# Strassen products in all three feed-forward blocks, their weight sums made by adding transfers

## The reference

```python
def conv_ffn(x, ln_g, up_w, conv_w, conv_b, down_w):          # blocks 0 and 1
    u = causal_dwconv(rms_norm(x, ln_g) @ up_w, conv_w, conv_b)   # 3 taps along the positions
    gate, up = u[..., :FFN_DIM], u[..., FFN_DIM:]
    return (jax.nn.silu(gate) * up) @ down_w

def swiglu(xn, w_gate, w_up, w_down):                          # block 2
    return (jax.nn.silu(xn @ w_gate) * (xn @ w_up)) @ w_down
```

## Time and profile before

| what | us |
|---|---|
| median of 3 runs | 2398.46 (2397.93 to 2400.35) |
| the profiled execution's own time | 2399.27 |
| its span | 2397.5 |
| PE busy | 2371.2 (99%) |
| DVE busy | 1484.8 (62%) |
| ACT busy | 1086.1 (45%) |
| POOL busy | 357.9 (15%) |
| transfers | 226.24 MB, mean 94 GB/s |

### The profile page before, as it was taken

One profiled execution on the slowest core, in us unless ns is written; L12 is line 12 of the kernel. 1 busy time (PEld: TensorE's weight loads), 2 busy tenths in 40 slices (PEclk: granted clock), 3 DMA queues, 4 the chain that ended last, 5 costly groups with the idle time before them and its releaser, 6 DMA issues.

```text
span 2397.5 us, 30764 instructions
## 1 busy us (share of the span) xinstructions
PE 2371.2 (99%) x11952; PEld 1944.2 (81%) x11952; DVE 1484.8 (62%) x2356; ACT 1086.1 (45%) x1878; POOL 357.9 (15%) x286
## 2 busy tenths in 40 slices
PE   8999999999999999999999999999999999999999
PEld 6677878888888877788888877787788878898987
DVE  6778776763666777766456547534655445873763
ACT  6654554442445677644234334324443334442433
POOL 0252252210111000122011100001210001100001
PEclk9999999999999999999999999999999999999999
DMA  4532223223223221232332332231234332233232
GB/s 164 109 93 79 80 70 99 97 86 108 97 83 120 75 76 49 73 108 92 93 106 87 91 131 84 71 102 57 72 123 136 115 106 79 81 105 99 95 97 89
DMA packets 74847, 226.24 MB, mean 94 GB/s; under 512 B 8144, under 2 KB 12368, under 8 KB 74576
## 3 DMA queue, kind: packets, MB, share of 16 engines
q1 hardware_dynamic: 70272, 215.90, 28.1%
q10 hardware_dynamic: 4432, 8.39, 2.0%
HBM read 215.87 MB, written 8.39 MB: 94 GB/s over the span
## 4 chain that ended last, share of the span: by engine, by line
PE 60%; DVE 1%; ACT 0%; issue 0%; DMA 0%; POOL 0%; POOLq 0%; DVEq 0%; ACTq 0%; SPq 0%
PE bank L1272 59%; PE bank L1276 1%; DVE t L2230 1%; DVE t L2233 1%; ACT t L1715 0%; DVE t L2241 0%; DMA t<-in_w 0%; POOL t L2877 0%; ACT t L1718 0%; ACT L1718 0%; DVE t L2237 0%; DVE t L2798 0%; POOLq L3100 0%; DVEq L3100 0%; DVE t L2644 0%
## 5 line engine op out<-in xcount | busy, mean ns | idle before, releaser
L1272 PE MATMUL bank<-t 128*128 128x512 f32 (+5 forms) x11526 | 2346.4, 369 | 19.1 <-DVE t L2233 7.9
L1272 PEld LDWEIGHTS bank<-t 128*128 128x128 f32 (+2 forms) x11526 | 1901.0, 186 | 433.3 <-issue 80.1
L1715 ACT ACTIVATE t<-t 128x1024 fp32r<-128x1024 f32 (+5 forms) x676 | 564.0, 847 | 564.6 <-PE bank L1272 276.6
L2230 DVE TENSOR_TENSOR t<-t 128x1024 fp32r<-128x1024 f32 (+7 forms) x774 | 687.3, 901 | 202.9 <-ACT t L1715 192.4
L1718 ACT ACTIVATE t<-t 128x512 f32<-128x512 f32 (+6 forms) x610 | 367.5, 616 | 455.8 <-DVE t L2230 307.1
L2877 POOL TENSOR_TENSOR t<-t 128x512 f32<-128x512 f32 (+4 forms) x206 | 316.3, 1542 | 1551.9 <-ACT t L1718 559.7
L2230 DVE TENSOR_TENSOR t<-bank,t 128x512 f32<-128x512 f32 (+4 forms) x434 | 279.2, 648 | 425.2 <-PE bank L1272 414.7
L2233 DVE SCALAR_TENSOR_TENSOR t<-t 128x512 f32<-128x512 f32 (+5 forms) x536 | 386.6, 733 | 102.3 <-ACT t L1718 63.8
L1715 ACT ACTIVATE t<-bank 128x512 f32<-128x512 f32 (+4 forms) x184 | 84.7, 477 | 205.4 <-PE bank L1276 146.9
L2880 POOL TENSOR_SCALAR t<-t 128x128 f32<-128x128 f32 (+3 forms) x64 | 40.9, 645 | 478.6 <-ACT t L1715 247.6
L2233 DVE SCALAR_TENSOR_TENSOR t<-bank,t 128x512 f32<-128x512 f32 x56 | 38.5, 688 | 68.8 <-PE bank L1272 68.8
(11 more groups left out here) (30 smaller groups left out, 53.0 us busy)
## 6 DMA issues: line engine op xcount, KB each, us to landing
t<-in_w SPq DMA_DIRECT2D x304, 512.0 KB, 3.4
t<-in_w SPq DMA_DIRECT2D x48, 384.0 KB, 3.0
t<-in_w SPq DMA_DIRECT2D x56, 320.0 KB, 3.0
t<-in_w SPq DMA_DIRECT2D x28, 256.0 KB, 2.8
tab<-t ACTq DMA_DIRECT2D x1, 2560.0 KB
t<-in_x SPq DMA_DIRECT2D x8, 256.0 KB, 5.0
t<-tab SPq DMA_DIRECT2D x8, 256.0 KB, 3.7
spill<-t ACTq DMA_DIRECT2D x1, 2048.0 KB, 8.3
```

The source lines that it names most:

```text
L1272: return eng.matmul(out, lhs, rhs, start=start, stop=stop, skip_group_check=loose)
L1715: return eng.activation(out, in_, ACT.Copy, scale=scale)
L2230: return eng.tensor_tensor(out, a, b, o)
```

## The change

- `QUADS` becomes a table: f = 9, 12, 14, 16, 18, 20 in blocks 0 and 1, and 10 of the 11 in block 2 (f = 5 becomes an ordinary pair). The sums of activations are made in each block (in XA for blocks 0 and 1).
- The order of the products becomes p1, p5, p6, p3, p7, p2, p4, and the four weight units are taken up at steps 0, 1, 3 and 5: first chunks (p1); s12 (p5, p6); s34 (p3, p7); last chunks (p2, p4). `cut_age` stays 2 throughout.
- Three of the four weight sums are made by transfers. A packed region of 128 x 2048 holds the four quarters. SP copies three of them (768 KB) into one of two buffers, 19 steps ahead (`base`). POOL issues a transfer that adds 512 KB from HBM into it, 15 steps ahead (`add1`), and one that adds 256 KB within SBUF, 9 steps ahead (`add2`). DVE makes the fourth sum, 128 x 512, 3 steps ahead (`add3`) in a buffer of its own, `sum4`. One of the two buffers is `scratch`, the memory of `acc` and `sqs`.
- The unit s34 lies in two buffers, so its `split` is two ACT copies of 512 elements and its `cut` two DVE subtractions of 512.
- In blocks 0 and 1 a Strassen pair's rows go through the taps; its results are multiplied by the row of norms on DVE, and gate times up is on DVE (11 steps after the pair's start; parts at 12 and 13).

```diff
-QUADS = (4, 5, 7, 8, 10, 12, 13, 15, 16, 18, 19)
-PRODUCTS = ("p1", "p2", "p6", "p5", "p7", "p3", "p4")
+QUADS = {0: (9, 12, 14, 16, 18, 20), 1: (9, 12, 14, 16, 18, 20), 2: (4, 7, 8, 10, 12, 13, 15, 16, 18, 19)}
+SUM_AGES = ((19, 15, 9, 3),) * 3
+PRODUCTS = ("p1", "p5", "p6", "p3", "p7", "p2", "p4")
+QUAD_HALF = {"p1": (0, 0), "p5": (1, 0), "p6": (1, 1), "p7": (2, 0), "p3": (2, 1), "p4": (3, 0), "p2": (3, 1)}
...
+        region = self.region((gate, 0, 4, gate_c + f * P, P), (up, 0, 4, up_c + f * P, P),
+                             (up, 4, 4, up_c + f * P, P), (gate, 4, 4, gate_c + f * P, P))
+        first = self.load(region, 0, S)
+        last = self.load(region, 2 * S, UNIT)
+        sources = (("raw", first, S), ("s12", (s, f), UNIT), ("s34", (s, f), UNIT), ("raw", last, UNIT))
         for i, product in enumerate(PRODUCTS):
-            if i % 2 == 0:
-                age, self.cut_age = self.cut_age, 1 if i == 4 else self.cut_age
-                u = self.ring(sources[i // 2])
-                self.cut_age = age
-                g.units.append(u)
-            self.put(Piece(g, i // 2, i, i + 1, i == 0))
+            if QUAD_HALF[product][0] == len(g.units):
+                g.units.append(self.ring(sources[len(g.units)]))
+            self.put(Piece(g, QUAD_HALF[product][0], i, i + 1, i == 0))
...
+        for name, age in zip(("base", "add1", "add2", "add3"), SUM_AGES[s]):
+            self.start(name, (s, f), t - age)
...
     def split(u):
-        copy(buf.his[u % N_W][:, 0:n], K.source(u)).then_inc(*sig["cut_hi"].up(u))
+        for a, b, of in K.source(u):
+            t = copy(buf.his[u % N_W][:, a:b], of)
+        t.then_inc(*sig["cut_hi"].up(u))
...
-            tt(buf.s1[:, S:UNIT], b[:, 0:S], b[:, S:UNIT], ADD).then_inc(*sig["sum1"].up(f))
-            tt(buf.s1[:, 0:S], a[:, 0:S], buf.s1[:, S:UNIT], ADD).then_inc(*sig["sum"].up(f, "s1"))
-            tt(buf.s2[:, 0:S], a[:, 0:S], b[:, 0:S], ADD)
-            tt(buf.s2[:, S:UNIT], a[:, S:UNIT], buf.s1[:, 0:S], ADD).then_inc(*sig["sum"].up(f, "s2"))
+            tt(buf.sum4[:, :], K.sums(sf)[:, 2 * S:3 * S], buf.raws[last % N_W][:, S:UNIT], ADD).then_inc(*sig["sum"].up(sf))
...
+    def adds(T):
+        for sf in at("add1", T):
+            region, *_ = plan.quad_units[sf]
+            i, turn, _ = K.sums_at(sf)
+            if turn > 1:
+                w.wait_ge(*sig.added[i][0].at(turn - 1))
+            w.wait_ge(*K.based(sf))
+            eng.dma_start(K.sums(sf)[:, 0:UNIT], K.region(region)[:, S:3 * S], accum_op=ADD).then_inc(
+                *sig.added[i][0].up())
+        for sf in at("add2", T):
+            i, turn, _ = K.sums_at(sf)
+            if turn > 1:
+                w.wait_ge(*sig.added[i][1].at(turn - 1))
+            w.wait_ge(*K.added(sf, 0))
+            eng.dma_start(K.sums(sf)[:, 2 * S:3 * S], K.sums(sf)[:, 0:S], accum_op=ADD).then_inc(*sig.added[i][1].up())
...
+    def base(sf):
+        region, *_ = plan.quad_units[sf]
+        i, turn, before = K.sums_at(sf)
+        if before:
+            w.wait_ge(*sig["cut"].at(plan.quad_units[before][4]))
+        elif i:
+            for j in range(4):
+                w.wait_ge(*sig["tee_lo"].at((sf[0], 3), j))
+        else:
+            w.wait_ge(*sig["lo"].at(*h_of(sf[0], 0)))
+        if turn > 1:
+            w.wait_ge(*sig.base[i].at(turn - 1))
+        eng.dma_start(K.sums(sf)[:, 0:3 * S], K.region(region)[:, 0:3 * S]).then_inc(*sig.base[i].up())
```

More of the change, by code:

```diff
@@ L293, in feat_steps, with quad @@
         self.pending.append(g)
[L295 to L299, removed]
+    def quad(self, s, f, gate, gate_c, up, up_c):
+        key = ("gu", s, f)
+        self.until(lambda: self.past("tees", (s, 3), 6 if f == QUADS[s][0] else SUM_AGES[s][0] + 4) and self.place(
+            [((*key, "b"), 0, 10), ((*key, "d"), 1, 6), ((*key, "a"), 5, 4)]), key)
@@ L528, in ffn @@
         late = 5 if s < 2 else 2
-        if s == 2:
-            for k in range(4):
-                self.once("tees", k, lambda k=k: self.past("rms", "n2", 3) and (k == 0 or self.past("tees", k - 1, 4)))
+        apart = 4 if s == 2 else 12
+        for k in range(4 if QUADS[s] else 0):
+            self.once("tees", (s, k), lambda k=k: self.past("rms", src, 3) and (
+                k == 0 or self.past("tees", (s, k - 1), apart)))
         self.start("ffn", s)
@@ L1114, in raw_read, with sums_at, sums, based @@
     def raw_read(self, r):
-        users = [u for u, (kind, n, _, _) in enumerate(self.plan.units) if kind == "raw" and n == r]
+        users = [u for u, (kind, n, _) in enumerate(self.plan.units) if kind == "raw" and n == r]
         done = [self.sig["cut"].at(u) for u in users]
-        for f, (first, *_) in self.plan.quad_units.items():
-            if r in (first, first + 1):
-                done.append(self.sig["sum"].at(f, "s2"))
-        return done
+        for sf, (_, last, *_) in self.plan.quad_units.items():
+            if r == last:
+                done.append(self.sig["sum"].at(sf))
+        return done
+    def sums_at(self, sf):
+        n, before = QUADS[sf[0]].index(sf[1]), [q for q in QUAD_LIST[:QUAD_LIST.index(sf)]]
+        turn = 1 + sum(QUADS[s].index(f) % 2 == n % 2 for s, f in before)
+        return n % 2, turn, (sf[0], QUADS[sf[0]][n - 2]) if n >= 2 else None
+    def sums(self, sf):
+        return self.buf.sums[self.sums_at(sf)[0]]
+    def based(self, sf):
+        i, turn, _ = self.sums_at(sf)
+        return self.sig.base[i].at(turn)
+    def added(self, sf, j):
+        i, turn, _ = self.sums_at(sf)
+        return self.sig.added[i][j].at(turn)
     def tee(self, i):
@@ L1308, in quads @@
         out = take(key)[:, 0:H2] if first else K.of(key)[:, 0:H2]
-        u, half = g.units[p.k0 // 2], p.k0 % 2
+        which, half = QUAD_HALF[product]
+        u = g.units[which]
         wh, wl = (t[u % N_W][:, half * S:half * S + S].rearrange("p (k n) -> p k n", k=4) for t in (buf.his, buf.los))
@@ L1936, in quads @@
[L1936 to L1946 removed]
+                copy(out, K.of(("gu", s, f, QUAD_BANK[product]))[:, 0:H2]).then_inc(*sig["q_copy"].up(s, f, product))
@@ L2287, in evacuate @@
             if s < 2:
-                if f >= 2 or (f == 1 and kind == "up"):
-                    w.wait_ge(*sig["tap"].at(("ga" if (n - 3) % 2 == 0 else "up", s, (n - 3) // 2), 2))
+                fu_free(n, s)
                 scaled(g, buf.fu[n % 3][:, 4:S + 4])
@@ new lines, in fu_free, with taps @@
+    def fu_free(n, s):
+        if n >= 3:
+            w.wait_ge(*sig["tap"].at(("ga" if (n - 3) % 2 == 0 else "up", s, (n - 3) // 2), 2))
+    def taps(key):
+        kind, s, f = key
+        n = 2 * f + (kind == "up")
+        ft = f + FFC * (kind == "up")
+        v, ub = buf.fv[n % 6], buf.fu[n % 3]
+        for k in (1, 2):
+            w.wait_ge(*(sig["tap0"].at(key) if k == 1 else sig["tap"].at(key, 1)))
+            stt(v[:, :], ub[:, 2 + k:S + 2 + k], pc(f"fcw{s}", 3 * ft + k), v[:, :], MUL, ADD).then_inc(
+                *sig["tap"].up(key, k))
@@ L3007, in gpsimd_program @@
         ssm(T)
+        adds(T)
         ffn(T)
@@ L3042, in sync_program @@
                 load(plan.units[u][1] + N_W)
+        for sf in at("base", T):
+            base(sf)
         for h in at("tb", T):
```

371 lines of the change are left out of this document (213 added, 158 removed).

## The result

| | before | after |
|---|---|---|
| median, us | 2398.85 (2397.93 to 2400.35, 4 runs) | 2432.97 (2429.82 to 2436.29, 4 runs) |
| ratio | | 1.0142, 95% interval 1.0124 to 1.0159 |
| the profiled execution's own time | 2399.27 | 2434.27 |
| its span | 2397.5 | 2432.2 |

The change makes the kernel 34.1 us slower. The direction was as predicted, the size three times the predicted 11.0 us, and 2433 lies outside the range (2390 to 2422). Two figures of the page after, against the earlier trace rows: PE's busy time should have fallen by 12 us and rose by 4.9; transfers by POOL's queue (the last line) are new.

A forecast was written before the change was run, and what follows sets the result against it. PE's own work was taken to bound the kernel; -12.1 + 5.5 + 0.4 + 15.2 + 2.0 = +11.0 us on 2399.3 gave 2410.3, or 2409.5 us as the median. The range was 2390 to 2422.

The forecast's parts named there:

- PE's own work: Strassen pairs of all blocks, 10.07 us against 10.90 for ordinary ones if nothing waits: -12.1 us.
- the sign that I had named: PE's busy time over the whole kernel falls by about 12 us while its idle time rises by over 20.
- The third weight unit: s34, needed at step 3 of each Strassen pair, comes late behind queued ACT and DVE work: 5.5 + 0.4 + 15.2 us.
- The rival in which the unit is covered after all: At s34, ACT and DVE reach it before other work, every pair waits only 0.15 us: 2389.7 us; chance 0.19.
- the one in which DVE is the bound: Blocks 0 and 1: DVE load alone makes eight pairs, f = 14 to 20, bring nothing: about 2393 us; chance 0.09.
- The second of two pairs: f = 8, 13, 16, 19: s12 ready at 1.95 us, needed at 1.44; 0.5 us each, 2.0 in all.
- The adding transfers: `base`, `add1`, `add2`: a 10.6 us chain fits the room of 17 to 21.8 us, so 0.
- the rival in which the adds land late: Adding transfers at 2.5 times plain time or more delay s12, 3 to 6 us per pair: 2425 to 2445; chance 0.08.
- Sums of activations: Blocks 0 and 1: 3.1 us of DVE and 1.9 of ACT per block, covered by spare time: 0.

The follow-up runs named there:

- x9: x1 with `add2` of block 2's second of two Strassen pairs issued later and DVE's `cut` for that pair's s12 one step earlier (all blocks): 2387.48 us, 0.9956.
- x1: Changed kernel with s34 earlier: ACT's `split` ahead of the copy of p1, DVE's `cut` one step earlier, ahead of the taps: 2391.38 us, 0.9972.
- x2: Changed kernel with gate times up of the ordinary pair before a Strassen pair, blocks 0 and 1, on DVE instead of POOL: 2418.31 us, 1.0085.
- x8: x1 without the two adding transfers, so its weight sums are incomplete: 2388.15 us, 0.9957.
- x3: Changed kernel with `add2` issued 6 steps ahead in place of 9 in all of block 2: 2447.37 us, 1.0203.
- x6: Changed kernel with only ACT's `split` of s34 early, DVE's `cut` at its old place behind the taps: 2429.36 us, 1.0134.
- x4: Changed kernel with both the edit of x1 and that of x3: 2404.96 us, 1.0028.
- x10: x9 with one further Strassen pair, f = 5, in block 2: 2394.91 us, 0.9992.

## Why the prediction was wrong

**1. PE's own work, -12.1: right.** x9, which has this work and none of the waits, is 12.9 us of span below before, 0.8 more than I summed. But the sign that I had named (PE busy down by 12) failed in the changed kernel, since work at a lower clock and the refills count as busy: -12.1 + 11.8 + 4.9 = +4.6, measured +4.9.

**2. The third weight unit: the right mechanism, the wrong price. This is the step that failed.** Its place, the order of the queues and 20 waits on DVE were right, and so were the 11.2 us of the single pairs of block 2 (11.27). The rival in which the unit is covered after all was wrong, and so was the one in which DVE is the bound, since x1 has no wait left in blocks 0 and 1. But the pairs of blocks 0 and 1 took 12.5 to 14.0 us and not 11.3 to 11.7. The step's 21.1 us (5.5 + 0.4 + 15.2) should have been about 47: 21.1 + 6.2 (waits of blocks 0 and 1 too short) + 3.9 (waits of block 2 too short) + 3.9 (refill, put at nothing) + 11.8 (clock, put at nothing) = 46.9.
- For blocks 0 and 1, I gave the `cut` 1.30 us behind taps that end at 4.3. The taps ended at 4.28, the `split` at 3.75; the `cut` took 2.4, because its second half meets POOL's product. I had the row for this and used it for the adding transfers, not here. In size: 10 x 1.07 = 10.7 us, by x2 and the changed kernel. The Trainium skill, "SBUF — State Buffer", section "Who interferes with whom", has the rule: a DVE instruction with two inputs in SBUF contends with a GpSimd instruction that reads SBUF. 1.75 us in place of 0.69 agrees with it. The prediction cited the section for the descriptors of the adding transfers alone. I had also let the wait grow to 1.6 for f = 14 to 20 by a backlog on DVE; it was the same 2.14 (and in x2 the same 1.07) for f = 9 as for the others, so that backlog does not exist.
- A wait costs more than its length: 0.26 us of refill each, 3.9 us for the 15 of this step. The rows had it: the first double of before takes 22.2 us with a wait of 1.7, where one without a wait takes 20.3.
- Behind 8 of the 12 waits of over 2 us the clock fell: 11.8 us. This I had not thought of. I had read the row of 9s as the full clock in every slice, which it does not say; in before the clock fell once between 1400 and 1500 us, where PE shows no wait at all:

```profile
1400.00:1500.00 100.00, 100.00 (x522) 77.11 (x521) 66.55 (x204) 43.92 (x112) 0.00 (x0) 0.98 0.24 77
```

- In block 2 the waits of f = 4 and 10 were 0.94 and 0.95 (predicted 1.1), but those of f = 15 and 18 were 2.22 and 3.82, by POOL's queue: 3.8 us more. My 4th step weighed when the adds land, and not who stands behind a POOL instruction that waits. f = 7 had 1.42; what of it is POOL's no run separates.

**3. The second of two pairs, 0.5 each: 0.3 each** plus 0.26 of refill, 2.2 us for the four against 2.0. The cause was as stated: x9 removes it by moving that `cut`.

**4. The adding transfers, 0: right for the transfers, wrong for their queue.** They land in 5.4 us (512 KB, `add1`) and 4.2 (256 KB, `add2`) at the median, where SPq's plain ones take 3.5 and 3.2; `base` takes 5.0 (predicted 4.4):

```profile
t<-in_w SPq DMA_DIRECT2D x282, 512.0 KB, 3.5
...
t<-in_w SPq DMA_DIRECT2D x22, 768.0 KB, 5.0
t<-in_w SPq DMA_DIRECT2D x50, 256.0 KB, 3.2
t<-in_w POOLq DMA_DIRECT2D x22, 512.0 KB, 5.4
t<-t POOLq DMA_DIRECT2D x22, 256.0 KB, 4.2
```

The chain of 14.6 us fits into the room of 17 to 21.8 that I had given, and by x8 it costs nothing that the runs can tell. So the measured 2433 us lies in the range of the rival in which the adds land late (2425 to 2445) by chance: without the adds (x8) the kernel is only 3.2 us faster than x1, and the longest waits of PE were for DVE. The estimate from the Trainium skill, "DMA: Bandwidth & Descriptors", section "Anatomy of one DMA", 3.2 and 2.6 us, is well below both.

**5. Sums of activations, 0: right.** In the changed kernel, the 384 matmuls of ordinary tiles between f = 9 and f = 12 take 87.07 us, 227 ns each, with the block's other stretches equally unbroken.

## What to carry to other kernels

When a unit of work is needed one step earlier, its place in each engine's queue must move too: count what stands ahead of it on every engine, and look at what the instruction ahead releases on others, since that runs at the same moment and may slow the unit down, as POOL's product did here (1.75 us in place of 0.69). An instruction that waits for a transfer holds up all that its engine has behind it, so a transfer's issue belongs on an engine's queue only where its wait is already over. Before a change of step counts is judged, compare the stages that it does not touch: here a parity in the planner was worth ten times a Strassen pair.

## What the runs showed of the hardware

- TensorE's granted clock fell from 2.4 to 1.2 GHz for a while behind some waits of 2.14 us inside a Strassen pair, and behind others of the same length, place and neighbours not: 6 of 10 in the changed kernel, 6 of 10 in x3, 4 of 10 in x6. Most cost 1.48 us (13.95 against 12.47 for the pair). In or behind the twelve waits of 2.2 to 6.0 us in block 2 (changed kernel, x2, x3, x4, x6, x10) it fell every time. Behind waits of 1.08 (ten in x2), of 0.95 and of 1.3 to 1.5 it never did in a profiled execution. What decides at 2.14 us stays open. The spread of the changed kernel's times goes with it: 2429.8 us at a mean clock of 0.996, 2436.3 at 0.992.
- DVE's subtraction of two SBUF tiles of 128x512 takes 0.69 us alone and 1.75 beside POOL's product of the same size; 128x1024 takes 1.22 alone and 2.31 in x1 beside POOL (1.29).
- An adding transfer took 1.3 to 1.5 times what a plain one from HBM of the same size took (4.2 against 3.2 us for 256 KB within SBUF, 5.4 against 3.5 for 512 KB from HBM), and its issue holds POOL 0.87 us.
